# Layer trunk on one core: twelve of the MLP down projection's sixteen groups become three blocks of seven products

## What is computed

```python
def squared_relu_mlp(h, w_up, w_down):
    return jnp.square(jax.nn.relu(h @ w_up)) @ w_down

for i in range(DEPTH):                      # DEPTH = 2
    h = rmsnorm(x, norm_mix[i])
    ...
    x = x + y
    h = rmsnorm(x, norm_mlp[i])
    x = x + squared_relu_mlp(h, w_up[i], w_down[i])
```

## Time and profile before

| | us |
|---|---|
| time, median of 3 runs (2622.96 to 2627.08) | 2626.74 |
| the profiled execution, its own time | 2626.96 |
| its span, first to last instruction | 2625.3 |
| TensorE busy | 2559.6 (97%) |
| VectorE busy | 1748.6 (67%) |
| ScalarE busy | 927.7 (35%) |
| GpSimd busy | 341.4 (13%) |

### The profile page before, as it was taken

The page is one execution under the profiler, slowest core; times in us unless marked ns, Lnnn a source line. Parts: engine busy times, 40 slices in busy tenths (PEclk is TensorE's granted clock), DMA queues, the critical chain, the costliest instruction groups (busy, mean ns, idle before and its releaser), DMA issues. The chain is left out here.

```text
span 2625.3 us, 36963 instructions
## 1 busy us (share of the span) xinstructions
PE 2559.6 (97%) x11929; PEld 2141.8 (82%) x11929; DVE 1748.6 (67%) x3103; ACT 927.7 (35%) x1732; POOL 341.4 (13%) x667
## 2 busy tenths in 40 slices
...
DMA packets 161730, 231.68 MB, mean 88 GB/s; under 512 B 21681, under 2 KB 103889, under 8 KB 161618
## 3 DMA queue, kind: packets, MB, share of 16 engines
...
## 5 line engine op out<-in xcount | busy, mean ns | idle before, releaser
L682 DVE TENSOR_TENSOR xT<-ps,xT 128x512 f32<-128x512 f32 x704 | 482.5, 689 | 266.1 <-PE ps L505 265.7
L503 PE MATMUL ps<-aT_hi,wd_hi 128*128 128x512 f32 x1408 | 552.7, 393 | 4.1 <-DVE wd_lo L453 4.1
L505 PE MATMUL ps<-aT_hi,wd_lo 128*128 128x512 f32 x1408 | 549.2, 390 | 0.0
L504 PE MATMUL ps<-aT_lo,wd_hi 128*128 128x512 f32 x1408 | 549.1, 390 | 0.0
L503 PE MATMUL ps<-bh,uw_hi 128*128 128x512 f32 x880 | 343.4, 390 | 5.6 <-DVE xn L880 2.5
L504 PE MATMUL ps<-bl,uw_hi 128*128 128x512 f32 x880 | 343.1, 390 | 0.0
L505 PE MATMUL ps<-bh,uw_lo 128*128 128x512 f32 x880 | 342.9, 390 | 0.0
L503 PEld LDWEIGHTS ps<-aT_hi,wd_hi 128*128 128x128 f32 x1408 | 265.1, 188 | 57.9 <-issue 4.5
L505 PEld LDWEIGHTS ps<-aT_hi,wd_lo 128*128 128x128 f32 x1408 | 264.9, 188 | 55.5
L504 PEld LDWEIGHTS ps<-aT_lo,wd_hi 128*128 128x128 f32 x1408 | 265.2, 188 | 54.0
L446 ACT ACTIVATE aT_hi<-raw 128x1024 fp32r<-128x1024 f32 x80 | 80.6, 1052 | 595.9 <-PE ps L505 582.3
...
## 6 DMA issues: line engine op xcount, KB each, us to landing
raw<-in_w_up SPq DMA_DIRECT2D x64, 512.0 KB, 5.5
raw<-in_w_down SPq DMA_DIRECT2D x64, 512.0 KB, 3.6
raw<-a_dram SPq DMA_DIRECT2D x64, 512.0 KB, 3.3
raw<-in_ret_w_in SPq DMA_DIRECT2D x48, 512.0 KB, 5.1
...
xT<-x_dram SPq DMA_DIRECT2D x24, 512.0 KB, 6.0
...
```

What stands on the lines that cost most here:

```text
L503: pe.matmul(bank, ah, bh, start=(begin and i == 0), stop=False, skip_group_check=not begin)
L504: pe.matmul(bank, ah, bl, start=False, stop=False, skip_group_check=not begin)
L505: last = pe.matmul(bank, al, bh, start=False, stop=(i == len(pairs) - 1), skip_group_check=not begin)
L682: dve.tensor_tensor(xT[:, k, cols], ps[:, banks[m % len(banks)], :], xT[:, k, cols], ALU.add).then_inc(x_add, 1)
```

## The change

Groups 0 and 1 stay as they are, and groups 14 and 15, the last 512 rows, are made as before under the numbers 2 and 3. The twelve between, 3072 rows, become three blocks of 1024 rows. In a block w_down is a 1024x1024 matrix A and a is a 1024x1024 matrix B, each cut into quarters of 512x512 (1 MB, a tensor 128 x 4 x 512): A11, A12, A21, A22, B11 and so on. Their product is made with seven products of quarters in place of eight. A product is 4 tiles m of 128 features by 512 tokens, each of 4 row pieces by 3 matmuls: 12 matmuls a tile, 48 a product.

Product n = 0 to 6 of a block takes the factors of `FACTOR`: A11 by B11, A12 by B21, AV by BV, AV by BV again with new contents, A21 by B12, A12 by B22, A22 by B21. AV, BV and, from products 4 and 5 on, A21, B12, A12, B21 hold sums (`TERMS`), four per side: GpSimd makes them (`blk_one`), each in two halves (`PARTS`) of 128x1024, 16 instructions a block. ScalarE splits hi (`op_hi_act`) and VectorE lo (`op_lo_dve`) of four pieces of 128x1024 for each product, into two sets of buffers `op` by n odd and even. Products 3 to 6 are summed onto what the PSUM bank already holds (`begin`), after VectorE has added that to `xT` (`op_add_dve`). Two sets of four banks take turns.

Each pair of quarters, (A11, B11), (A21, B12), (A12, B22), (A22, B21), counts its loads on one semaphore, and who waits for one quarter of a pair waits for both. SyncE loads B11 and B21 of block 0 after group 0, B12 and B22 after group 1, since they lie where those groups' buffers are; later blocks' quarters follow as their places come free.

Elsewhere some semaphores are merged (`pos_mm` into `gT_mm`, `o_tr` into `n_tr` and the like), with waits for the matching counts.

```diff
 PAIRS = MLP_GROUPS // 2
+BLOCKS = 3
+PARTS = 2
+POOL_SIDES = "AB"
+DN = MLP_GROUPS - 4 * BLOCKS
+PRODUCTS = 7 * BLOCKS
...
+        op_hi, op_lo = {}, {}
+        for i in range(2):
+            with place(32 * i) as z:
+                for side in "AB":
+                    op_hi[side, i] = sb(f"op{side}_hi{i}", [P, 4, HALF], F32R, z)
+                    op_lo[side, i] = sb(f"op{side}_lo{i}", [P, 4, HALF], F32R, z)
+        blk = {}
+        for kb, names in ((64, ("B11", "B21")), (112, ("B12", "B22", "AV", "BV")), (146, ("A11", "A12", "A21", "A22"))):
+            with place(kb) as z:
+                for name in names:
+                    blk[name] = sb(f"blk{name}", [P, 4, HALF], F32, z)
...
+        blk_in = {}
+        for pair in (("A11", "B11"), ("A21", "B12"), ("A12", "B22"), ("A22", "B21")):
+            blk_in[pair[0]] = blk_in[pair[1]] = sem(f"blk_in_{pair[0]}_{pair[1]}")
+        blk_sum = {side: sem(f"blk_sum{side}") for side in "AB"}
...
+            k = (2 * g if g < 2 else 2 * g + 8 * BLOCKS) + j % 2
+            src = a_k[:, k:k + 1, :] if j < 2 else wd[:, k:k + 1, :]
...
-            if not (isinstance(g, int) and g < 2) and j == 0:
+            if g == 2 and j == 0:
+                act.wait_ge(op_mm, 4 * product_at(layer, PRODUCTS - 1))
+            if g == 2 and j == 2:
+                act.wait_ge(op_lo_s, 2 * PARTS * product_at(layer, PRODUCTS))
+            if g > 2 and j == 0:
                 act.wait_ge(down_mm, TILES * (DG_D[layer] + g - 1))
...
+        def sum_value(layer, n, v, h):
+
+            return 4 * PARTS * (BLOCKS * layer + n // 7) + PARTS * (v - 1) + h + 1
...
+        def lo_value(layer, n, h, side):
+
+            return 2 * PARTS * product_at(layer, n) + 2 * h + "AB".index(side) + 1
...
+        FACTOR = {"A": ("A11", "A12", "AV", "AV", "A21", "A12", "A22"),
+                  "B": ("B11", "B21", "BV", "BV", "B12", "B22", "B21")}
+        SUM_OF = {"A": (0, 0, 1, 2, 3, 4, 0), "B": (0, 0, 1, 2, 3, 0, 4)}
+        ON_FIRST = (0, 3, 4, 6)
+        RESULT = ((0, 0), (0, 0), (1, 1), (0, 1), (1, 1), (0, 1), (1, 0))
+        BEHIND = (2, 2, 1, 3, 1, 3, 2)
...
+        def op_bank(n, m):
+            first = n % 7 in ON_FIRST
+            return (4 if first == (n // 7 % 2 == 0) else 0) + m
...
+        def blk_load(sp, layer, b, name):
+            side, i, j = name[0], int(name[1]) - 1, int(name[2]) - 1
+            wd = w_down[layer].rearrange("(k p) n -> p k n", p=P)
+            k = 4 + 8 * b + 4 * (j if side == "A" else i)
+            c = HALF * (i if side == "A" else j)
+            apart(sp)
+            sp.dma_start(blk[name][:], (wd if side == "A" else a_k)[:, k:k + 4, c:c + HALF]).then_inc(blk_in[name], 16)
+
+        def blk_arrived(eng, layer, n, name):
+            eng.wait_ge(blk_in[name], 32 * (BLOCKS * layer + n // 7 + 1))
+
+        def op_hi_act(act, layer, n, h, side):
+            if (h, side) == (0, "A"):
+                if n == 1:
+                    act.wait_ge(down_mm, TILES * (DG_D[layer] + 1))
+                if n > 1:
+                    act.wait_ge(op_mm, 4 * product_at(layer, n - 1))
+            name, v = FACTOR[side][n % 7], SUM_OF[side][n % 7]
+            if v:
+                act.wait_ge(blk_sum[side], sum_value(layer, n, v, h))
+            else:
+                blk_arrived(act, layer, n, name)
+            act.activation(op_hi[side, (n + 1) % 2][:, piece_of(h), :], part(name, h), ACT.Copy).then_inc(op_hi_s, 1)
...
+        def op_lo_dve(dve, layer, n, h, side):
+            dve.wait_ge(op_hi_s, lo_value(layer, n, h, side))
+            dst, hi = (t[side, (n + 1) % 2][:, piece_of(h), :] for t in (op_lo, op_hi))
+            dve.tensor_tensor(dst, part(FACTOR[side][n % 7], h), hi.bitcast(F32), ALU.subtract).then_inc(op_lo_s, 1)
...
+        OP_PIECES = [(h, side) for h in range(PARTS) for side in "AB"]
+
+        def op_add_dve(dve, layer, n, m):
+            i, j = RESULT[n % 7]
+            dst = xT[:, 4 * i + m, j * HALF:(j + 1) * HALF]
+            dve.wait_ge(op_mm, 4 * product_at(layer, n) + m + 1)
...
+            dve.tensor_tensor(dst, ps[:, op_bank(n, m), :], dst, ALU.add).then_inc(op_add, 1)
...
+        def op_pe(pe, layer, n):
+            pe.wait_ge(op_lo_s, 2 * PARTS * product_at(layer, n + 1))
+            for m in range(4):
+                if n == 1:
+                    pe.wait_ge(x_add, TILES * (DG_D[layer] + 2) - 3 + m)
+                elif n > 1:
+                    pe.wait_ge(op_add, 4 * product_at(layer, n - BEHIND[n % 7]) + m + 1)
+                i, c = (n + 1) % 2, slice(m * P, (m + 1) * P)
+                product(pe, ps[:, op_bank(n, m), :],
+                        [(op_hi["A", i][:, k, c], op_lo["A", i][:, k, c], op_hi["B", i][:, k, :], op_lo["B", i][:, k, :])
+                         for k in range(4)], begin=n % 7 < 3).then_inc(op_mm, 1)
+
+        TERMS = {("A", 1): ("AV", "A21", "A22", ALU.add), ("A", 2): ("AV", "AV", "A11", ALU.subtract),
+                 ("A", 3): ("A21", "A11", "A21", ALU.subtract), ("A", 4): ("A12", "A12", "AV", ALU.subtract),
+                 ("B", 1): ("BV", "B12", "B11", ALU.subtract), ("B", 2): ("BV", "B22", "BV", ALU.subtract),
+                 ("B", 3): ("B12", "B22", "B12", ALU.subtract), ("B", 4): ("B21", "B21", "BV", ALU.subtract)}
+
+        def blk_one(eng, layer, b, side, v, h):
+            n0 = 7 * b
+            dst, x, y, op = TERMS[side, v]
+            for name in (x, y):
+                if name[1] != "V":
+                    blk_arrived(eng, layer, n0, name)
+            if v == 1 and b:
+                eng.wait_ge(op_lo_s, lo_value(layer, n0 - 4, h, side))
+                eng.wait_ge(blk_sum[side], sum_value(layer, n0 - 7, 4, h))
+            elif v == 1:
+                eng.wait_ge(down_mm, TILES * (DG_D[layer] + 2))
+            else:
+                eng.wait_ge(blk_sum[side], sum_value(layer, n0, 2 if v == 4 else 1, h))
+            if v == 2:
+                eng.wait_ge(op_lo_s, lo_value(layer, n0 + 2, h, side))
+            if v == 4:
+                eng.wait_ge(op_lo_s, lo_value(layer, n0 + 1, h, side))
+            eng.tensor_tensor(part(dst, h), part(x, h), part(y, h), op).then_inc(blk_sum[side], 1)
+
+        def down_pool(pool, layer):
+            for b in range(BLOCKS):
+                for v in (1, 2, 3, 4):
+                    for h in range(PARTS):
+                        for side in POOL_SIDES:
+                            blk_one(pool, layer, b, side, v, h)
...
         def down_pe(pe, layer, tile_done):
             dn_pe(pe, layer, 0, 2)
-            with pe.Fori(0, MLP_GROUPS // 2 - 1) as gg:
-                dn_pe(pe, layer, 2 * gg + 1, 1)
-                dn_pe(pe, layer, 2 * gg + 2, 2)
+            dn_pe(pe, layer, 1, 1)
+            for n in range(PRODUCTS):
+                op_pe(pe, layer, n)
+            dn_pe(pe, layer, 2, 2)
             dn_pe(pe, layer, D_LAST, 1, tile_done, range(TILES if tile_done else FILLED))
...
-            with act.Fori(1, MLP_GROUPS // 2) as gg:
-                for b in range(2):
-                    for j in range(4):
-                        dn_hi_act(act, layer, 2 * gg + b, j, D_BUF[b])
-
-        def dn_dve(dve, layer, g, b):
+            for n in range(PRODUCTS):
+                for h, side in OP_PIECES:
+                    op_hi_act(act, layer, n, h, side)
+            for g in (2, 3):
+                for j in range(4):
+                    dn_hi_act(act, layer, g, j, D_BUF[g % 2])
...
-            dn_dve(dve, layer, 0, 1)
-            with dve.Fori(0, MLP_GROUPS // 2 - 1) as gg:
-                dn_dve(dve, layer, 2 * gg + 1, 2)
-                dn_dve(dve, layer, 2 * gg + 2, 1)
+            low = lambda g, j: lambda: dn_lo_dve(dve, layer, g, j, D_BUF[g % 2])
+            op_low = lambda n, i: lambda: op_lo_dve(dve, layer, n, *OP_PIECES[i])
+            dn_dve(dve, layer, 0, {5 + 2 * j: low(1, j) for j in range(4)})
+            dn_dve(dve, layer, 1, {6 + 2 * i: op_low(0, i) for i in range(2 * PARTS)})
+            for n in range(PRODUCTS):
+                todo = [low(2, i) if n == PRODUCTS - 1 else op_low(n + 1, i)
+                        for i in range(4 if n == PRODUCTS - 1 else 2 * PARTS)]
+                for i, w in enumerate(todo):
+                    w()
+                    if i == len(todo) // 2 - 1:
+                        op_add_dve(dve, layer, n, 0)
+                for m in range(1, 4):
+                    op_add_dve(dve, layer, n, m)
+            dn_dve(dve, layer, 2, {4 * j: low(3, j) for j in range(4)})
             last_adds()
 
         def down_sp(sp, layer):
-            with sp.Fori(2, MLP_GROUPS) as g:
-                for j in range(4):
-                    dn_load(sp, layer, g, j)
+            sp.wait_ge(u_mm, ub(layer, PAIRS - 1) + OPS)
+            for name in ("A11", "A12", "A21", "A22"):
+                blk_load(sp, layer, 0, name)
+            for j in range(4):
+                dn_load(sp, layer, 2, j)
```

(48 more changed lines are left out.)

54 lines of the change are left out of this document (31 added, 23 removed).

## The result

Five runs of each kernel: 2611.24 us median after (2610.32 to 2612.87), 2622.96 before (2622.53 to 2627.08). The ratio is **0.9949, 95% interval 0.9937 to 0.9962** (the two medians alone would give 0.9955). The forecast was 2608 us, range 2572 to 2631. By the ratio, 0.9949 of the 2626.7 that I started from, the change is worth 13.4 us (10.0 to 16.5); I had forecast 19.1. By the two profiled executions it is 2625.3 - 2611.1 = 14.2.

What follows compares the result with a forecast made beforehand. TensorE was taken as the bound, busy 97% of the span. From 2626.74 us, -65.3 for removed matmuls and +46.2 for waits and lower clock gave -19.1: 2608 us, range 2572 to 2631.

Steps and rivals of the forecast that it cites:

- What goes, -65.3: Down stage: 336 matmuls a block in place of 384, 10.88 us less, six blocks, -65.3 us.
- the code of the products, written out and put at nothing: TensorE's code for the products, written out in place of a loop, was taken to cost nothing.
- A turn of 3.35 us: Beside products, VectorE lows and GpSimd sums alternate, 3.35 us for one of each, 13.4 us per product against 10.88.
- whole instructions added up (3.54): Alternative turn length without overlap of low and sum: 3.54 us a turn, 14.2 a product, total 13 us higher.
- Which products wait: TensorE waits for lows before products 3, 4, 10, 11, 17, 18, 1.7 to 2.5 us each, 13.3 us per layer.
- The wait for B22, 7.8: Product 1 waits for B22's late load through the shared semaphore, 7.8 us once per layer.
- rival B: Late loads hold up sums in later blocks and product 1, 2670 us, slower than before; chance 0.13.
- 46.2: All forecast losses in the down stage over two layers: 2 x (13.3 + 7.8 + 2) us.
- The six short waits: TensorE's waits before products 3, 4, 10, 11, 17, 18, forecast at 13.3 us per layer.
- The clock's 2 us per layer: TensorE's clock drops after the wait before product 1, costing 2 us per layer.
- Rival C: The clock also falls at the twelve 2.5 us waits, 2 us each, +24, 2632 us; chance 0.12.
- Rival A: ScalarE's rounding spaces the lows, sums hide between them, only B22's landing counts, 2570 us; chance 0.15.

Runs made afterwards that it cites:

- e4: Changed kernel with all sums on VectorE, none on GpSimd, and A12 counted with B21, A22 with B22: 0.9750 of the kernel before, 2559.08 us.
- e5: Changed kernel with each GpSimd sum of 128x1024 written as two instructions of 128x512: 0.9903 of the kernel before.
- e9: e4 plus four unneeded GpSimd fills of 128x1024, reading nothing, beside the lows of products 6, 7, 13 and 14 each: 0.9751 of the kernel before.
- e8: e4 plus four unneeded GpSimd copies of 128x1024, one SBUF input, beside the lows of products 6, 7, 13 and 14 each: 0.9750 of the kernel before.
- e2: Changed kernel with GpSimd sums 2, 3 and 4 made over half their columns, the other half left out: 0.9834 of the kernel before.
- e1: Changed kernel with other semaphore pairs, A12 counted with B21 and A22 with B22: 0.9967 of the kernel before.
- e6: Changed kernel with GpSimd sums in two 128x512 instructions, and A12 counted with B21, A22 with B22: 0.9899 of the kernel before.
- e3: Changed kernel with all sums made by VectorE and GpSimd doing nothing in the stage: 0.9801 of the kernel before.

## Why the prediction was nearly right

**What goes, -65.3.** Right. e4, which has the same products and no wait, gains 65.7. It also shows that the code of the products, written out and put at nothing, costs nothing that can be measured.

**A turn of 3.35 us.** Right: 3.34 in the rows. The Trainium skill, SBUF — State Buffer, section "SBUF: two separate sides", calls the shared ports an exclusive lock and no split of bandwidth; e5's shorter lows (2.31 for 3.41) agree. Against a VectorE instruction with two SBUF inputs, the same section of the Trainium skill limits this to GpSimd instructions that read SBUF, and the fill of e9 beside the copy of e8 agrees. With whole instructions added up (3.54) product to product would be 14.2; it was 13.34.

**Which products wait.** Right, all six and no other, and e2 shows that it is the length of the sums that makes them wait. Their sizes in later blocks: forecast 1.7 and 2.5, measured 2.25 and 2.54 in the rows. Of the first difference 0.42 is a step I had left out: the rounding starts not with the product but 0.42 us later (product 9 at 1348.42, its first rounding at 1348.84), once the last matmul before it is done. In the first block 2.4 and 2.5 were forecast and 3.23 and 0.96 seen, the second short because the clock had fallen in the product before it and that product's matmuls took up 1.5 us of it.

**The wait for B22, 7.8.** Right in kind (e1 and e4 take it away), 8.3 and 8.6 in size. The rounding began 8.1 us into product 0, where I had 8.6:

```profile
1243.25 1.06 ACT L1297 ACTIVATE opA_hi<-blkA 128x1024 fp32r<-128x1024 f32 x1 [17.42 <-DMA blkB<-a_dram]
```

The loads were about as forecast, so rival B had no ground: 1 MB landed in 5.0 us (A) and 7.1 (B) in the median, and no product 8 or 9 waited. That the wait was longer all the same is one hold more than I had walked through: a sum was already under way when the first low came (1244.34), which took 2.17 us for that. What I did not see is what else the pairs do. A22 counts with B21, which is loaded last, and so the next block's first sums start late enough to miss most of the lows of products 7 and 14. I named the wait for B22 as a loss of its own, and as such it was worth 7.9 and 7.1 us in e1; but that edit also lets the first sums start early, and so as a whole it brings nothing.

**Where the 4.7 us between 46.2 and 50.9 are.** They are in the size of three terms, read from how far products overran 10.88 us. Product 0 overran by 8.3 and 8.6 us, forecast 7.8 each: 1.3 more. The six short waits of a layer made their products overrun by 15.0 and 14.7 us, forecast 13.3 each: 3.1 more. The lower clock cost 1.5 and 1.8 us in product 1 and 1.5 in product 18 of layer 0, forecast 2 per layer: 0.8 more. The products behind a short wait gave some 0.4 back. The idle times alone, 22.1 and 20.5 us beside 21.1 forecast, agree better than the account does, since a lower clock hid some of the waiting.

**The clock's 2 us per layer** rested on a wrong reading. I took the 11 of the earlier trace rows for matmuls that started in 4 us. It counts all that ran in the stretch, which are 20 in 4 us at full clock. In the trace of the kernel before, the weight loads of that place stand 0.43 us apart:

```profile
704.12 0.33 PEld L504 LDWEIGHTS ps<-aT_lo,wd_hi 128*128 128x128 f32 x1
704.55 0.33 PEld L505 LDWEIGHTS ps<-aT_hi,wd_lo 128*128 128x128 f32 x1
```

So some 9.4 start in 4 us, and by the loads from 702.8 to 708.4 the gap cost 2.6 us, not 2. That 1.5 and 1.8 came in the changed kernel is near my 2 by luck.

**Rival C came true in part.** The granted clock fell behind four of the twelve short waits (3.23 and one of 2.54 in layer 0, 2.92 and one of 2.25 in layer 1). It was 0.66 to 0.70 over the five us there, with weight loads 0.43 us apart for part of them, which is the lower of the clock's two levels, 1.2 and 2.4 GHz. Each time it cost 1.5 us of matmuls. Waits of 2.25 and 2.54 stand on both sides of this, and in e6 the clock stayed at 1.00 behind 3.27 and 3.29 in layer 0 and fell behind 3.29 in layer 1; in no run did I find what decides it. Three of the four cost nothing, because the next product was bound by its lows anyway and its wait shrank from 2.5 to 0.96; the fourth, behind 1455.58, came in the last products with no wait ahead of them and cost its 1.5.

**Rival A** had the wrong premise that roundings space the lows: beside sums they took 3.41 us. But e3, where no sum stands against a low, shows what it would have been worth: 2574 us, where I had 2570.
